# A mixture-of-experts stage: token rows scattered to their experts' slots ahead, and loaded by plain transfers

## What is computed

```python
# hier_moe(h): group top-1, expert top-2 of 32 experts, SwiGLU experts
g_top, g_idx = lax.top_k(softmax(x @ w_rg + b_rg), 1)
e_in_group = take((x @ w_re + b_re).reshape(NT, 4, 8), g_idx)
e_top, e_idx = lax.top_k(softmax(e_in_group), 2)
weights = g_top * e_top / sum(e_top)
expert = g_idx * 8 + e_idx
# every token goes to its two experts:
gate, up = split(x_rows @ w_e_in[e])            # 1024 -> 2 x 512
y_rows = (silu(gate) * up) @ w_e_out[e]         # 512 -> 1024
y[token] += y_rows * weight
```

## Time and profile before

| | us |
|---|---|
| median of 3 runs (lowest to highest) | 1806.08 (1802.74 to 1806.83) |
| profiled execution | 1807.53 |
| its span | 1805.7 |
| TensorE busy in the span | 1682.9 (93%) |
| VectorE, ScalarE, GpSimd busy | 1014.3, 442.2, 235.0 |
| bytes moved | 334.20 MB, mean 185 GB/s |
| gathers of x: issues, median from issue to landing | 32, 11.1 us |

### The profile page before, as it was taken

How to read it: one execution, slowest core, us unless ns; L and a number is a source line. 1 busy time by engine, 2 the same in 40 slices (tenths; PEclk the granted TensorE clock), 3 DMA queues, 4 the chain that set the end, 5 groups by cost and what they waited for, 6 DMA issues and landing times.

```text
span 1805.7 us, 35644 instructions
## 1 busy us (share of the span) xinstructions
PE 1682.9 (93%) x14825; PEld 932.5 (52%) x14825; DVE 1014.3 (56%) x2446; ACT 442.2 (24%) x1072; POOL 235.0 (13%) x359
## 2 busy tenths in 40 slices
PE   5999999999999999999999999969999998989890
PEld 3455444544445554555545545546777555555550
DVE  2486526564565345444444435556777777676754
ACT  5121323334443222222212311012222121212110
POOL 3030000000111122220222230010000000000003
PEclk9999999999999999999999999979999999999995
DMA  9377200001112011010110472368999999999997
GB/s 345 118 265 247 67 24 24 24 24 47 47 47 79 19 33 33 16 33 19 33 33 15 177 288 101 129 207 321 378 399 400 393 396 386 396 392 395 390 367 297
DMA packets 105413, 334.20 MB, mean 185 GB/s; under 512 B 13594, under 2 KB 57544, under 8 KB 93036
## 3 DMA queue, kind: packets, MB, share of 16 engines
q1 hardware_dynamic: 86256, 282.70, 42.2%
q0 software_dynamic: 8240, 25.04, 4.1%
q10 hardware_dynamic: 10828, 25.24, 3.9%
HBM read 299.51 MB, written 37.63 MB: 187 GB/s over the span
## 4 chain that ended last, share of the span: by engine, by line
PE 79%; DMA 14%; DVE 3%; issue 1%; POOL 1%; ACT 1%; SPq 1%; ACTq 0%; POOLq 0%; DVEq 0%
PE bank L296 77%; DMA arena<-in_w_e_in 10%; DMA arena<-in_w_e_out 2%; DMA arena<-in_w_in 1%; POOL arena L768 1%; PE bank L954 1%; DMA arena<-y_slots,ints 1%; SPq L378 1%; DVE arena L2390 0%; DVE arena L1884 0%; PE bank L1242 0%; DMA arena<-in_kn_g_c 0%; ACTq L1416 0%; DVE arena L2380 0%; DMA arena<-xnorm,ints 0%
## 5 line engine op out<-in xcount | busy, mean ns | idle before, releaser
L296 PE MATMUL bank<-arena 128*32 128x256 f32 (+9 forms) x14446 | 1641.0, 390 | 54.8 <-DMA arena<-in_w_e_in 21.7
L296 PEld LDWEIGHTS bank<-arena 128*32 128x32 f32 (+3 forms) x14446 | 887.3, 132 | 777.8 <-issue 562.4
L2380 DVE STREAM_TRANSPOSE arena<-arena 32x256 f32<-32x256 f32 x372 | 161.9, 435 | 5.7
L2390 DVE STREAM_TRANSPOSE arena<-arena 32x128 f32<-32x128 f32 x384 | 157.7, 411 | 4.8
L1734 ACT ACTIVATE arena<-bank 128x128 f32<-128x128 f32 x96 | 19.7, 278 | 420.9 <-PE bank L296 420.9
L2371 DVE TENSOR_TENSOR arena<-bank,arena 128x512 f32<-128x512 f32 x64 | 35.5, 558 | 103.3 <-PE bank L296 103.3
L1726 ACT ACTIVATE arena<-arena 128x96 f32<-128x96 f32 x248 | 92.1, 461 | 5.2 <-DVE arena L2380 5.2
L730 POOL DMA_INDIRECT arena<-xnorm,ints x32 | 31.4, 981 | 464.8 <-DVE arena L2380 446.7
L2141 DVE TENSOR_TENSOR arena<-arena,bank 128x128 f32<-128x128 f32 (+1 forms) x40 | 11.4, 286 | 130.3 <-PE bank L296 130.3
L681 POOL TENSOR_TENSOR arena<-arena 64x256 f32<-64x256 f32 x96 | 70.2, 731 | 30.3 <-DVE arena L2117 23.7
L1884 DVE RECIPROCAL arena<-arena 128x512 f32<-128x512 f32 x10 | 33.5, 3348 | 31.9 <-ACT arena L1471 31.9
(11 more groups left out here) (339 smaller groups left out, 1037.5 us busy)
## 6 DMA issues: line engine op xcount, KB each, us to landing
arena<-in_w_e_in SPq DMA_DIRECT2D x64, 2048.0 KB, 27.0
arena<-in_w_e_out SPq DMA_DIRECT2D x32, 2048.0 KB, 27.4
arena<-in_w_ada SPq DMA_DIRECT2D x12, 2048.0 KB, 12.9
arena<-in_w_in SPq DMA_DIRECT2D x32, 512.0 KB, 4.0
y_slots<-arena ACTq DMA_DIRECT2D x32, 288.0 KB, 9.4
y_slots<-arena POOLq DMA_DIRECT2D x21, 384.0 KB, 17.8
arena<-in_w_in SPq DMA_DIRECT2D x3, 2048.0 KB, 21.7
arena<-in_x SPq DMA_DIRECT2D x4, 1024.0 KB, 8.5
```

Of the source, the lines that this page charges most:

```text
L296: return nc.tensor.matmul(o, l, r, start=start, stop=stop)
L2380: ins = V.transpose(e_xT[s][ts(b, QT), :, ts(t, QT)], rows[:, :, b, :])
L2390: ins = V.transpose(hT[ts(q, QT), :, ts(t, QT)], e_h[ts(c, QT), r, :].rearrange("p (n k) -> p k n", k=4))
```

## The change

The slot of each token row is known when its tile is placed, so the rows are written to their slots in a DRAM tensor `x_slots` (32 x 96 rows) as soon as each tile is through:

- `place` works out the slot number of each token for both of its experts (rank over 96: out of bounds) instead of the one-hot; `table` and the conversion are gone. GpSimd issues two indirect DMAs per tile, which scatter the 128 rows of `o_n` to `x_slots`.
- VectorE waits, before it overwrites `o_n`, for the scatters of the tile that used the buffer.
- `x_slots` is first filled with finite values: three copies of the input x, 4 MB each, DRAM to DRAM, issued by ScalarE ahead of the attention stage.
- The gathers are gone. SP loads the 96 rows of an expert by one plain transfer, in the same queue as the weights. Load 0 and 1 wait for all scatters; load e+2 waits for `xs_used`. Each stands ahead of a second half of input weights.
- The clearing of the buffers is gone; a ScalarE branch in the expert loop becomes a last turn written out.

```diff
@@ sync
+            def load_x(e, s):
+                sp.dma_start(e_xs[s][0:CAP, :], xs_b[ds(e, 1)].rearrange("o p n -> (o p) n")).then_inc(sem(f"xs{s}_in"), 16)
+
             third(0)
-            sp.wait_ge(sem("xs0_in"), 16)
+            for s in range(2):
+                sp.wait_ge(sem(f"x_sc{s}"), 16 * NT)
+            load_x(0, 0)
+            load_x(1, 1)
+            sp.wait_ge(sem("xs_used"), 1)
+            load_x(2, 0)
             third(1)
+            sp.wait_ge(sem("xs_used"), 2)
+            load_x(3, 1)
...
             next_in(3, 0, 1)
+            sp.wait_ge(sem("xs_used"), 3)
+            load_x(4, 0)
             next_in(4, 1, 2)
             next_out(3, 0, 1)
             next_out(4, 1, 2)
...
+            def two(i, last=False):
+                sp.wait_ge(sem("win_half"), 2 * i - 1)
+                w_in_half(2 * i, 1, 0)
+                sp.wait_ge(sem("win_used"), 2 * i - 1)
+                sp.wait_ge(sem("xs_used"), 2 * i)
+                load_x(2 * i + 1, 1)
+                w_in_half(2 * i, 1, 1)
                 next_out(2 * i - 1, 0, 2 * i - 2)
-                next_in(2 * i + 1, 0, 2 * i)
+                sp.wait_ge(sem("win_half"), 2 * i)
+                w_in_half(2 * i + 1, 0, 0)
+                sp.wait_ge(sem("win_used"), 2 * i)
+                if not last:
+                    sp.wait_ge(sem("xs_used"), 2 * i + 1)
+                    load_x(2 * i + 2, 0)
+                w_in_half(2 * i + 1, 0, 1)
                 next_out(2 * i, 1, 2 * i - 1)
@@ gpsimd
-            gather(0, 0, False)
-            gather(1, 1, False)
-            with pool.Fori(1, NE // 2) as i:
...
+            pool.wait_ge(sem("vecs_in"), 16 * (len(vec_rows) + X_FILLS))
+            for t in range(NT):
+                pool.wait_ge(sem("x_placed"), t + 1)
+                for a in range(TOPK):
+                    n = TOPK * t + a
+                    pool.indirect_dma_start(out=xslot_d, out_offset=bass.IndirectOffsetOnAxis(ap=i_dst[:, n:n + 1], axis=0),
+                                            in_=o_n[t % 2], in_offset=None,
+                                            bounds_check=NE * CAP - 1, oob_is_err=False)\
+                        .then_inc(sem(f"x_sc{t % 2}"), 16)
@@ scalar
             act.wait_ge(sem("b_silu"), 4)
+            for n in range(X_FILLS):
+                act.dma_start(xslot_d[T * n:T * n + T], I["x"][0]).then_inc(sem("vecs_in"), 16)
             keys(0)
             attn_p(0)
@@ vector, place
-                if t >= 2:
-                    dve.wait_ge(sem("r_tab"), t - 1)
                 rank = rank_bank(t).unsqueeze(1).to_broadcast([P, TOPK, NE])
                 link(TT(r_t, r_m[:, t], rank, ALU.mult))
-                TS(r_in[:, t % 2], r_m[:, t], r_tok[:, t:t + 1], None, ALU.mult)
                 link(V.tensor_reduce(out=r_rank[:, t], in_=r_t, axis=AX, op=ALU.add))
-                TT(r_hot[:, t % 2], r_iP.unsqueeze(1).to_broadcast([P, TOPK, P]), bc(r_rank[:, t], P), ALU.is_equal)\
-                    .then_inc(sem("r_hot"), 1)
+                STT(r_slot, r_v[:, t], -float(CAP), r_rank[:, t], ALU.mult, ALU.add)
+                link(TS(r_far, r_rank[:, t], float(CAP), float(8 * T), ALU.is_ge, ALU.mult))
+                STT(i_dst[:, TOPK * t:TOPK * t + TOPK], r_slot, float(NE * CAP), r_far, ALU.add, ALU.add)\
+                    .then_inc(sem("x_placed"), 1)
@@ vector, tile loop
                 if t >= 2:
                     dve.wait_ge(sem(f"xn_st{t % 2}"), 16 * (t // 2))
+                    dve.wait_ge(sem(f"x_sc{t % 2}"), 32 * (t // 2))
```

## The result

The changed kernel has a median of 1827.2 us over all its 8 runs; two of them, 1846.65 and 3585.7, were slow ones and are in no comparison, and the other six have a median of 1825.1 (1810.81 to 1829.73; the five others start at 1821.97). The kernel before, beside it on the chip, has 1806.53 in 8 runs (1802.74 to 1809.48). The ratio, that of the mean times, is 1.0094, 95% interval 1.0068 to 1.0119. The profiled execution took 1823.1 us with a span of 1821.3, which is 15.6 us over the 1805.7 of before. The forecast was 1812.0 with a range to 1820: the sign was right, the size was not, and the range didn't hold it.

The account below looks back on a forecast made before the run. TensorE was taken to bind the router stage, and DMA most of the expert stage from 1395.38 to 1717.70 us. -2.0 + 0.8 + 4.1 + 3.0 = +5.9 us, on the median 1812.0; range 1804 to 1820.

Parts of the forecast that it names:

- Router stage, tables removed: Router stage: TensorE binds, so 6 passes without the table product save 0.33 us each, -2.0 us, at worst 0.
- The wait of the scatters and the hand-over: Router's end: VectorE waiting to overwrite o_n, +0.8 (0 to +3); scatter then load before expert 0, +4.1 (+1.4 to +7).
- SP's queue: Expert stage: loads of x among the weights; in the DMA-bound part no wait for xs_used, x 5 us early: nothing.
- rival B: Serial hops or a late x decide: scatter wait +3, hand-over +7, bytes +6, less 2: +14, 1820 us; chance 13%.
- Fills: Before the router's end, near 261 us: three 4 MB copies inside DRAM beside gate weights; likely 0, up to +10 us.
- Rival D: The fills collide with the gate weights' loads: +10 us more, 1822 us; chance 5%.
- DMA work of an expert: DMA-bound expert stage: plain loads carry all 96 rows, 5.5 us more if paid in full; half taken, +3.0 (0 to +7).
- A: Expert stage: uneven engines hide the added bytes, so only +2.9 us remains, 1809 us; chance 15%.
- C: Expert stage: mixing gathers in slows the stream; removing them returns -9 us over 18 experts, 1803 us; chance 13%.
- The doubt about the base rate: Expert stage: C's case that the stream speeds up without gathers, pointing to faster, 1803 us; chance 13%.

Follow-up runs that it names:

- e1: Changed kernel with each plain load of x cut from 96 rows to rows 0 to 63 (256 KB): 1818.05 us, ratio 1.0067.
- e2: Changed kernel with the same 384 KB per load of x written as 128 partitions of 3 KB: 1776.58 us, ratio 0.9835.
- e3: Changed kernel without the loads of x for experts 2 to 31, SP's waits kept: 1775.97 us, ratio 0.9826.
- e7: Changed kernel with loads of x widened to 128 rows, each in two transfers of 64 partitions: 1873.83 us, ratio 1.0377.
- e8: Changed kernel with loads of x of 96 partitions by 3 KB, last 256 columns left out (288 KB): 1803.41 us, ratio 0.9985.
- e9: Changed kernel with the same 96-row plain loads issued by GpSimd in its own queue, SP keeping its waits: 1814.01 us, ratio 1.0038.
- e5: Changed kernel with each load of x widened from 96 to 128 rows and partitions (512 KB): 1784.44 us, ratio 0.9883.
- e4: Kernel before with empty slots' indices held at the last token, so each gather moves all 96 rows: 1809.33 us, ratio 1.0013.
- e6: Kernel before with each gather over 128 indices and partitions instead of 96: 1782.74 us, ratio 0.9872.
- e11: Kernel before without the gathers of experts 2 to 31, waits on the first gather only: 1775.43 us, ratio 0.9829.
- e10: Changed kernel with 128-row loads of x, each in two transfers of 128 partitions by 2 KB: 1788.04 us, ratio 0.9896.

## Why the prediction was wrong

**Router stage, tables removed: right.** -2.0 was forecast; the first product of tile 7 is 1188.19 - 1185.83 = 2.4 us earlier, and the five whole passes that had a table in them fell from 16.42 to 15.97.

**The wait of the scatters and the hand-over: right in kind, half the size.** +0.8 and +4.1 were forecast. From the first product of tile 7 to the transposes it was 1211.16 - 1188.19 = 23.0 us and is 1210.95 - 1185.83 = 25.1: +2.1 for both. The scatter landed in 3.50 us where I had put 5.1. The estimate from the Trainium skill, DMA: Bandwidth & Descriptors, "Anatomy of one DMA" (3.2 and 2.9 us for the two hops, about +2 in all), was nearer than mine; the hops measured 3.50 and 3.27. The section gives its formula for DMAs that GpSimd issues, so for the second hop, issued by SP, it was stretched. VectorE's wait for a scatter, from the source view of L761 of after (who waited, us, times; then landing):

```profile
  DVE arena L2298: 1.6, 1
...
DMA to landing us min/median/max: 3.3/6.0/9.3
```

It is one wait of 1.6 us. It can be more, as the prediction said it might. In six of the ten profiles with this router stage (e1, e2, e3, e7, e8, e9) a scatter begun near 1180, about when SP issues the 2 MB block, took 6.74 to 7.82 us and was on the chain. In e3, for one:

```profile
1182.11 7.39 DMA x_slots<-arena,ints
```

There the transposes started at 1214.78, 3.8 us after those of after, so one pair of profiles is not enough for this part: the level hand-over of after holds for that execution. Over after and its variants that load x by one transfer from SP (e1, e2, e3, e5, e8) they started at 1209.28 to 1214.78, on average 1211.9; over before and its variants (e4, e6, e11) at 1210.40 to 1212.57, on average 1211.7. So up to the hand-over the change cost some 0.3 us where -2.0 + 0.8 + 4.1 = +2.9 was forecast. Together the two steps stay inside the sum of their ranges (+1.4 to +10).

**SP's queue: right that no load of x came late, wrong in "no wait" and in "nothing".** The loads took a median of 24.3 us to land, and the only one who ever waited for one was TensorE, for expert 0 (source view of L508):

```profile
  PE bank L1324: 9.2, 1
...
DMA to landing us min/median/max: 3.3/24.3/27.2
```

The late x of rival B didn't come. But SP did wait for `xs_used` in the DMA-bound part, where turning the rows was to end 1.5 us ahead of the products (its waits from 1300 to 1760: us, times, longest):

```profile
SPq L556 <- DVE arena L2398: 58.0, 12, 5.3
SPq L564 <- DVE arena L2398: 56.8, 12, 5.2
```

That is 4.8 us a time. By themselves these waits cost nothing: e3 has 122.5 us of them and is at the floor. What was put at nothing and wasn't is the loads' place between the weights, some 10 us by e9.

**Fills: right.** From 260 to 300 the engines moved 365 and 321 GB/s, and TensorE worked 16.16 and 20.00 us of 20, as the windows above show. Rival D is out, and e3 against e11 (1775.97 and 1775.43) agrees with that.

**DMA work of an expert: this step failed.** The prediction took the rate that the queues showed, 24.7 GB/s an engine, as what an engine does, and asked only how many more bytes there would be: 5.5 us if paid in full, half of it taken. e4 put the same bytes on the gathers and they cost 2 us: this sum was about right for what it counted. But 24.7 was no property of the engines. It was already the slowed rate: with no x moved the same queue goes at 26.5 (e11), and with x over 128 partitions at 26.6 (e5). What sets it is above all the shape of the transfers mixed in, and the change kept the 96 partitions and made it worse: plain rows, all with bytes, between the weights of one queue. By the table x cost 31 us before and 48 after, 17 more where +3.0 was forecast; 15 of them show between the two profiles. Of the 17, e4 gives 2 to the bytes and e9 some 10 to the queue, and 5, little more than the intervals leave open, lie between e4 and e9: a gather against a plain load of 96 rows, and SP's waits for `xs_used`, which e9 has too. One sum in this step was off as well: the window held 23 gathers, not 24, and 9.05 MB in place of 9.44 make a full price of 4.5 us where it says 5.5; the miss doesn't come from that.

**The rivals.** A said that engines are unevenly loaded and the new bytes are therefore free. Against it stood the mean share of 1.01 for all sixteen. In e4 the bytes cost 2.3 us of a full price of 4.5 to 5.5, so something of A may be in it; no run tried that, and it is no part of the loss. C came nearest to the cause: it saw 419 GB/s of 4 KB rows alone against 393 of the mixed stream and wrote that mixing in slows the stream. It then gave this to the *gather* as a kind of DMA, and so expected a gain from its removal. e6 refutes that: the gather stays, only its width changes, and 23 of its 31 us come back. C's own row spoke against it: in that last stretch most of the bytes were gathers too, those of the result rows, over 128 indices each. The queue of gathers in before from 1790 to 1800:

```profile
q0 software_dynamic: 692, 2.49, 61.0%
```

That is 2.49 MB of the 4.19 that moved at 419 GB/s. Had C asked what else sets the gathers of x apart from the weights, the kernel had it: 96 rows beside blocks of 128 partitions. The doubt about the base rate was there, with 13 in 100, and in no case did it point to slower. B's 1820, the nearest number, is no hit: neither the hops nor a late x made the loss.

**What was tried of the cause, and what is open.** That the partitions of a transfer into SBUF decide most of the cost is shown, by e2 against e8, by e10 against e7 and by e6 against before. Why they do isn't: the trace doesn't tell the 16 engines apart. The Trainium skill, DMA: Bandwidth & Descriptors, "The descriptor swizzle", says that in a transfer of 128 partitions each engine writes to the partitions of one SBUF port, eight of them, and "Where 436 GB/s comes from" that the 16 ports give 435 GB/s and are the bottleneck; the 427 to 429 of e2, e3, e5 and e11 agree with that. In "Why a DMA increments its semaphore by 16 and not by 1" it says that 96 or 64 partitions too go over all 16 engines, which leaves six or four to each. If these are dealt out in order, an engine would write across ports whose own engines are busy with weights, and both would wait. It fits 128 partitions against fewer, and the slower packets at a full share; it was only argued, and it doesn't say why 3 KB rows cost so much less than 4 KB ones. Open too is why the same 96 rows cost some 10 us more in SP's queue than in GpSimd's (after against e9), beyond that the extra wait is for output weights. The Trainium skill, in the same page's section "Issuing engines are not separate DMA queues", says that issuing from several engines saves only the time of the issue; here more than that changed, and the measurement decides, for this case.

## What to carry to other kernels

Where the DMA engines bind, look at the partitions of every transfer into SBUF that runs beside the big stream, and try each at 128, even if that moves a third more bytes: here e5 and e6, with 128 for 96, are by the ratios 38 us faster than after and 23 faster than before, the kernels that they come from, and e6 is one edited line. A rate read from a profile is the rate of that mixture: before bytes are multiplied by it, compare a stretch in which one kind of transfer runs alone. And where a small stream hides behind a large one and nobody waits for it, the run without it (e11) tells what it costs.

## What was not expected of the hardware

- Transfers of 96 partitions that make up 4 to 6% of the bytes took 427 GB/s down to 389 to 400 from 1600 to 1700, and two of 64 to 366, with the DMA share at 1.01 each time.
- One core alone moved 429 GB/s from 1600 to 1700 in e3 and e11, and 428, 427 and 428 GB/s in e5's windows from 1300, 1500 and 1600, with the stores to `y_slots` in it, which leave from 96 partitions (288 KB an expert) and from 32 (96 KB): in this direction those widths left the stream at 429.
- A gather's cost hardly hangs on its bytes: 53% more of them (5.92 to 9.05 MB, e4) cost 2 us, and 32 more indices for an expert, nearly all of empty slots (e6), gained 23.
- Copies of 12.6 MB inside DRAM beside the gate weights' loads, at 365 GB/s with them, cost TensorE nothing: it was busy 16.16 us from 260 to 280 and 20.00 us from 280 to 300, and before the change 16.08 and 20.00.
